# Layer 2's gates and branch products computed with tokens on the partitions, and turned back on the way into the output projection

## The reference

```python
def hybrid_layer(x, layer, norm_w, w_in, ..., w_branch, w_out, rel_bias):
    h = rms_norm(x, norm_w)
    p = h @ w_in                     # z, gate (4 x 2048 columns), the branches' inputs
    ...                              # four attentions of 4 heads: dsa, fox, diff, dilated
    for b in range(N_BRANCHES):      # 4
        y = branches[b].reshape(...) * jax.nn.silu(z_parts[b])          # 256 x 512
        term = jax.nn.sigmoid(g_parts[b]) * (y @ w_branch[b])           # 256 x 2048
        merged = term if merged is None else merged + term
    return x + merged @ w_out
```

## Time and profile before

| | |
|---|---|
| median of 3 runs | 2753.43 us (2752.55 to 2753.89) |
| span of the profiled execution | 2751.3 us, first to last instruction; what lies around it in a run is, by the median, 2.1 us; no other time is given for the profiled execution itself |
| PE busy | 2732.2 us, 99% of the span |
| PEld, DVE, ACT, POOL busy | 87%, 69%, 46%, 2% |
| TensorE's granted clock | 0.999 of full speed over the span |
| gates and what runs beside them | 2173.0 to 2557.3 us |
| 16 branch blocks | 2557.3 to 2649.4 us |
| 16 blocks of the projection | 2649.4 to 2738.8 us |

### The profile page before, as it was taken

The page is one execution under the profiler, slowest core; times in us unless marked ns, Lnnn a source line. Parts: engine busy times, 40 slices in busy tenths (PEclk is TensorE's granted clock), DMA queues, the critical chain, the costliest instruction groups (busy, mean ns, idle before and its releaser), DMA issues.

```text
span 2751.3 us, 40122 instructions
## 1 busy us (share of the span) xinstructions
PE 2732.2 (99%) x15856; PEld 2406.5 (87%) x15856; DVE 1898.5 (69%) x2111; ACT 1268.7 (46%) x1210; POOL 63.6 (2%) x113
## 2 busy tenths in 40 slices
PE   9999999999999999999999999999999999999998
PEld 8888888888888888888888888888888888888997
DVE  8685666777667879877777455765555766776686
ACT  6455457634645545544444333433333344443442
POOL 0000000000000000000000000000000000000100
PEclk9999999999999999999999999999999999999999
DMA  7764444565466555555555655555554566557853
GB/s 272 229 228 165 159 159 162 183 206 191 167 216 233 216 202 194 191 189 184 194 187 193 220 199 185 202 185 197 184 195 175 179 202 203 197 191 242 285 214 137
DMA packets 109476, 544.20 MB, mean 198 GB/s; under 512 B 11405, under 2 KB 25742, under 8 KB 54064
## 3 DMA queue, kind: packets, MB, share of 16 engines
q1 hardware_dynamic: 100128, 510.95, 53.0%
q0 software_dynamic: 9232, 31.57, 3.2%
HBM read 523.50 MB, written 23.04 MB: 199 GB/s over the span
## 4 chain that ended last, share of the span: by engine, by line
PE 91%; DVE 4%; ACT 2%; DMA 2%; issue 0%; SPq 0%; DVEq 0%; ACTq 0%
PE gemm L679 40%; PE gemm L682 21%; PE mix L679 6%; PE mix L1050 4%; PE mix L682 3%; PE gemm L733 2%; PE mix L1048 2%; PE gemm L735 2%; PE gemm L734 2%; DMA raw<-wstream 2%; DVE wlo L1726 2%; PE gemm L1050 1%; PE mix L657 1%; PE mix L656 1%; PE mix L655 1%; ACT whi L1228 1%
## 5 line engine op out<-in xcount | busy, mean ns | idle before, releaser
L1228 ACT ACTIVATE whi<-raw 128x2048 fp32r<-128x2048 f32 x466 | 891.2, 1913 | 1177.0 <-DMA raw<-wstream 1173.9
L1726 DVE TENSOR_TENSOR wlo<-raw,whi 128x2048 fp32r<-128x2048 f32 x465 | 1064.6, 2290 | 385.3 <-ACT whi L1228 384.2
L679 PE MATMUL gemm<-HX,whi 128*128 128x512 f32 x4864 | 1185.1, 393 | 2.0 <-DVE scratch L1751 0.7
L679 PEld LDWEIGHTS gemm<-HX,whi 128*128 128x128 f32 x4864 | 894.0, 188 | 174.4 <-issue 3.0
L682 PEld LDWEIGHTS gemm<-HX,wlo 128*128 128x128 f32 x4864 | 624.7, 191 | 21.5
L682 PE MATMUL gemm<-HX,wlo 128*128 128x256 f32 x4864 | 631.9, 283 | 0.0
L1751 DVE TENSOR_REDUCE arena<-gemm 128x256 f32<-128x512 f32 (+1 forms) x129 | 88.9, 689 | 177.6 <-PE gemm L679 177.4
L1050 PE MATMUL mix<-ACTX,whi 128*128 (+1 forms) x528 | 138.6, 392 | 0.3
L1050 PEld LDWEIGHTS mix<-ACTX,whi 128*128 128x128 f32 x528 | 97.0, 188 | 22.0 <-DVE XR L2312 2.9
L733 PE MATMUL gemm<-whi,HX 128*128 128x512 f32 x256 | 101.6, 397 | 1.6 <-DVE arena L1886 1.6
L679 PE MATMUL mix<-UX,whi 128*128 128x512 f32 x416 | 101.6, 392 | 0.0
(11 more groups left out here) (423 smaller groups left out, 2530.7 us busy)
## 6 DMA issues: line engine op xcount, KB each, us to landing
raw<-wstream SPq DMA_DIRECT2D x462, 1024.0 KB, 4.8
scratch<-gate_scratch POOLq DMA_DIRECT2D x12, 512.0 KB, 5.3
raw<-wstream SPq DMA_DIRECT2D x10, 512.0 KB, 6.2
gate_scratch<-scratch SPq DMA_DIRECT2D x32, 128.0 KB, 4.6
GL<-gate_scratch POOLq DMA_DIRECT2D x8, 512.0 KB, 5.3
gate_scratch<-arena SPq DMA_DIRECT2D x32, 128.0 KB, 4.7
bias_scratch<-row_scratch POOLq DMA_DIRECT2D x21, 192.0 KB, 5.2
raw<-wstream SPq DMA_DIRECT2D x12, 256.0 KB, 8.0
```

What stands on the lines that cost most here:

```text
L679: return pe.matmul(bank.rearrange("p (c t) -> p c t", c=2), whi[slot][:, w(k)], mx(k), start=k == 0, stop=k == total - 1)
L1228: f(whi[slot][:, :], raw[slot][:, :], ACT.Copy).then_inc(s["hi_ready"], 1)
L1726: tt(wlo[slot][:, :], raw[slot][:, :], whi[slot][:, :].bitcast(F32), ALU.subtract).then_inc(s["lo_ready"], 1)
```

## The change

The 64 gate blocks become 16 value groups: group k gives 512 features with tokens on the partitions, in banks `gate_bank`, which are the two gemm banks for even k and banks 4 and 5 of `M` for odd k. DVE copies a group's two banks out after its fourth block, and SP stores them in `gate2_d` as two transfers of 256 KB.

The 16 branch blocks also have tokens on the partitions (`YH` and `YL` stationary, 24 matmuls of 512 columns), and go by column quarters: quarter q is the four branches' blocks 4q to 4q + 3. So the gates come back in that order too (`gate2_back`), and a quarter of `merged` is complete after each fourth block. It then has tokens on the partitions, and the projection wants features there. DVE transposes its 32 x 32 blocks (two `transpose` instructions into `turned`), SP writes the four strips of 32 partitions to the scratch tensor `turn_d` in four transfers of 128 KB, waits until they have landed, and reads them back rearranged into `laid` (512 KB). ACT makes the high part of it (`turned_high`) and DVE the low part (`turned_low`), both beside the second block of the next quarter. Tokens then lie in the order strip, half, place; the moving operands of the projection are read in runs of 64, and DVE puts the tokens right as it adds the projection to the residual. The projection starts with three blocks taken together, chunks 0 to 11 first, then 12 to 15.

Cut to its core:

```diff
@@ V_GROUPS, stream_index
+V_GROUPS += tuple(range(B_G2, B_Y2, 4))
...
+    if isinstance(n, int) and B_Y2 <= n < B_O2:
+        return B_Y2 + N_Y2 * ((n - B_Y2) % 4) + (n - B_Y2) // 4
@@ sync
+            def strips(q):
+
+                sp.wait_ge(s["mg_t"], q + 1)
+                if q:
+                    sp.wait_ge(s["mg_l"], N_Y + q)
+                for a in range(4):
+                    sp.dma_start(turn_d[q, a].rearrange("b j x -> j b x"),
+                                 turned[32 * a:32 * a + 32, :].rearrange("j (b x) -> j b x", b=4)).then_inc(s["mg_out"], 16)
+                sp.wait_ge(s["mg_out"], 64 * (q + 1))
+                sp.dma_start(laid.rearrange("p (a x) -> p a x", a=4), turn_d[q].rearrange("a b j x -> (b j) a x")).then_inc(s["mg_in"], 16)
...
-            blocks(sp, B_G2, 4 * N_G, spill(1, 2 * N_G, use(B_G2)))
-            blocks(sp, B_Y2, N_BLOCKS - RING - B_Y2, reload)
+            for n in range(B_G2, B_Y2 + 1):
+                reload(n, n % RING, n // RING, 0, 0)
+                if n > B_G2 and (n - B_G2) % 4 == 0:
+                    spill2((n - B_G2) // 4 - 1)
+            for n in range(B_Y2 + 1, B_O2):
+                reload(n, n % RING, n // RING, 0, 0)
+                if (n - B_Y2) % 4 == 3:
+                    strips((n - B_Y2) // 4)
+            blocks(sp, B_O2, N_BLOCKS - RING - B_O2, reload)
@@ gpsimd
+            for i in range(4, 4 * N_Y2):
+                pool.wait_ge(s["y2_out"], i - 3)
+                gate2_back(i)
+                if i >= 12:
+                    pool.dma_start(XT2[:, quarter(i - 12), :], x2_d[:, quarter(i - 12), :]).then_inc(s["x2_back"], 16)
@@ tensor, values
-                    if b == 0:
-                        pe.wait_ge(s["evac_done"], u + t - 1)
-                    bank = gps[(u + t) % 2][:, :].rearrange("p (c f) -> p c f", c=4)
+                    if b == 0 and gate != 1:
+                        pe.wait_ge(s["evac_done"], u + t - (1 if gate < 1 else 3))
+                    if b == 0 and g == B_SUMS2:
+                        pe.wait_ge(s["head_rstd"], 4)
+                    bank = (gps[(u + t) % 2][:, :] if gate < 0 else gate_bank(g, t)).rearrange("p (c f) -> p c f", c=4)
@@ tensor, branch blocks
-                for c in range(4):
+                wh = whi[n % RING][:, :].rearrange("p (c k f) -> p k c f", c=4, k=4)
+                wl = wlo[n % RING][:, :].rearrange("p (c k f) -> p k c f", c=4, k=4)
+                for t in range(2):
+                    bank = M[:, 2 * (i % 2) + t, :].rearrange("p (c f) -> p c f", c=4)
                     for k in range(4):
-                        kk = 4 * (i // N_Y2) + k
-                        ins = mm3(M[:, 2 * (i % 2) + c // 2, (c % 2) * T:(c % 2 + 1) * T], cols(c * 4 + k),
-                                  YH[:, kk, :], YL[:, kk, :], n % RING, k == 0, k == 3)
+                        kk = 4 * (i % 4) + k
+                        yh, yl = YH[:, kk, cols(t)], YL[:, kk, cols(t)]
+                        pe.matmul(bank, yh, wh[:, k], start=k == 0, stop=False)
+                        pe.matmul(bank, yl, wh[:, k], start=False, stop=False)
+                        ins = pe.matmul(bank, yh, wl[:, k], start=False, stop=k == 3)
...
-            pair(B_O2, s["mg_l"], [(N_Y + i + 1, 4 * i + 4) for i in range(N_Y2)], hk, xk)
-            project(B_O2 + 2, N_O - 3, hk, xk)
+            for sem, k0, k1 in ((N_Y + 3, 0, 12), (N_Y + 4, 12, KT)):
+                pe.wait_ge(s["mg_l"], sem)
+                for b in range(3):
+                    ...
+                    ins = group(out_bank(b), range(k0, k1), KT, cols, hq, xq, n % RING, strips=True)
+            project(B_O2 + 3, N_O - 4, hq, xq, strips=True)
@@ scalar
+            for i in range(4 * N_Y2):
+                plain(B_Y2 + i, 1)
+                if 2 <= i < 4 * N_Y2 - 2:
+                    gate2(i + 2)
+                if i % 4 == 1 and i > 4:
+                    turned_high(i // 4 - 1)
+            plain(B_O2, 1)
+            turned_high(3)
@@ vector
+                if n == 3:
+                    if q:
+                        dve.wait_ge(s["mg_out"], 64 * q)
+                    ...
+                    for t in range(2):
+                        ins = dve.transpose(dst[:, t], src[:, t])
+                    ins.then_inc(s["mg_t"], 1)
...
+            for i in range(4 * N_Y2):
                 gated(i)
+                if i % 4 == 1 and i > 4:
+                    turned_low(i // 4 - 1)
                 plain(B_Y2 + i, 1)
-            for i in range(3 * N_Y2, 4 * N_Y2):
-                gated(i)
-                if i > 3 * N_Y2:
-                    merged_low(N_Y + i - 3 * N_Y2, 16, i - 3 * N_Y2 - 1, 4)
-                if i == 4 * N_Y2 - 1:
-                    merged_low(N_Y + N_Y2, 16, N_Y2 - 1, 4)
-                plain(B_Y2 + i, 1)
+            turned_low(3)
```

More of the change, by code:

```diff
@@ L693, in group, with project @@
                 return ins
-            def project(n0, count, mh, ml, fresh=None):
+            def project(n0, count, mh, ml, fresh=None, strips=False):
                 u0 = use(n0)
@@ L708, in body @@
                             pe.wait_ge(fresh[0], fresh[1] + q + 1)
-                        ins = group(gps[bank][:, :], ks, KT, cols, mh, ml, slot)
+                        ins = group(gps[bank][:, :], ks, KT, cols, mh, ml, slot, strips)
                     ins.then_inc(s["gemm_done"], 1)
@@ L735, in values @@
                         ins = pe.matmul(bank, xh, wl[:, k], start=False, stop=kk == KT - 1)
-                    if b == 3 and t == 0:
+                    if b == 3 and t == 0 and gate < 0:
                         ins.then_inc(s["v_half"], 1)
@@ L1786, in to_gates, with gate_values, take, to_ring @@
                 join(gates[0:56, :], gps[(u0 + j) % 2][0:56, :]).then_inc(s["evac_done"], 1)
-            def to_ring(layer, began):
+            def gate_values(k):
+                def take(n, u0, i, j):
+                    if n % 4 != (B_G2 + 3) % 4:
+                        return
+                    dve.wait_ge(s["gemm_done"], n + 1)
+                    for t in range(2):
+                        if k:
+                            dve.wait_ge(gate2_out[t], 16 * k)
+                        dve.tensor_copy(gring2[t], gate_bank(B_G2 + 4 * k, t)).then_inc(s["evac_done"], 1)
+                return take
+            def to_ring(began):
                 def take(n, u0, i, j):
@@ L2523, in _ @@
             dve.wait_ge(s["x2_back"], 64)
-            plain(B_O2, N_O, use(B_O2), residual(3, XT2), 3)
+            no_squares()
+            plain(B_O2, 3, use(B_O2), residual(3, XT2), 3)
+            plain(B_O2 + 3, N_O - 3, use(B_O2 + 3), residual(3, XT2, 3), 3)
             d = XT2[:, KT - 1, :]
```

176 lines of the change are left out of this document (112 added, 64 removed).

## The result

The median after the change is 2766.66 us (5 runs, 2765.01 to 2768.54), beside it before the change 2753.89 us: the ratio is 1.0047, 95% interval 1.0035 to 1.0060. The change makes the kernel 0.47% slower. The forecast was 2756 us, with a range that ended at 2766. The profiled execution took 2766.08 us, its span 2764.3 us.

A forecast was written before the change was run, and what follows sets the result against it. PE, busy 99% of the span, was taken as the bound. A gain of 13.4 us and waits of 16.1 us summed to +2.7: span 2754.0 us, median 2756.1, range 2746 to 2766.

The forecast's parts named there:

- the four places named: Where PE was to wait: branch blocks 8 and 12, the projection's start and its second pass.
- The gain: PE's gate blocks 8.3 us and branch blocks 5.1 us shorter, 13.4 us in sum.
- The transposes: DVE's two transposes per quarter, taken as 1.4 us, done 4.2 us after the quarter's fourth block.
- SP's stand: SP's four writes after the transposes, 0.35 us apart until 5.3, landed at 7.2 us after block 3.
- The load behind it: Weight load for block 8 goes out at 7.6 us, not 5.7, takes 7, not 5.0, landed at 14.7.
- PE's waits: PE waits 1.8 us before branch block 8, 4.9 before block 12, 2.4 before the projection.
- the 20.1 + 5 us of DVE a quarter: Branch blocks: DVE's work plus its standstill before the low part, 25 us per 21.8 us of PE.
- The clock: After long PE waits matmuls run at half speed, 0.45 us each, 4 to 5 us in all.
- rival 3: Slower by PE's half clock after waits, 4 to 5 us, 2760 to 2761; chance 0.12.
- After it: Projection: waits of 0.5 and 1.9 us at second and third block, 2.7 second pass, 1.9 fourth block.
- Rival 2: Slower by DMA crowding in the branch blocks: loads take 9 us, not 7, landing beyond 17; 2763; chance 0.25.
- Rival 1: The gain stays: DVE fits in the branch blocks, only a last chain of 3 to 5 us; 2744; chance 0.20.

The follow-up runs named there:

- e17: The changed kernel with four useless 512-column matmuls behind each of branch blocks 4 to 14, 10.0 us of PE work; 2766.7 us, ratio 1.0051.
- e4: The changed kernel with 12, 12, 8 and 8 useless matmuls ahead of PE's waits at branch blocks 8 and 12, projection start and second pass; 2766.4 us.
- e9: e8 with the last trip by SP, the third quarter's low part behind the last transposes, and the projection's first blocks in three passes; 2747.7 us, ratio 0.9982.
- e8: The changed kernel with the whole trip in POOL's queue and the high and low part one block later; 2755.6 us, ratio 1.0009.
- e7: The changed kernel with SP's next load ahead of its wait and read, and the high and low part one block later; 2760.1 us, ratio 1.0027.
- e16: The changed kernel with POOL's four residual pieces moved from the third quarter to the last one and after; 2766.3 us, ratio 1.0051.
- e14: The changed kernel with write wait and read by POOL (three quarters), later high/low parts, three projection passes, fourth projection block's split earlier; 2751.9 us, ratio 0.9997.
- e3: The changed kernel without transposes and trip through DRAM, high and low parts made from the merged quarter as it lies; 2745.5 us, ratio 0.9972.
- e5: The changed kernel with the whole trip (writes, wait, read) in POOL's queue, SP keeping the weight loads alone; 2762.2 us, ratio 1.0039.

## Why the prediction was wrong

The mechanism was right: the trip delays the load, ACT's high part and DVE's low part in this order, and PE waits at the four places named. Its sizes were not, and the one that failed is the time of the writes, 3.0 us a quarter. Each step against what was measured:

- **The gain.** Value matmuls stood 0.227 us apart, and the branch stage began at 2549.4 us, 7.9 earlier (forecast 8.3). Of the 5.1 us of the branch blocks only the first four's 1.3 shows: from block 4 on PE isn't on the chain, and in e17 10 us of extra work there cost nothing.
- **The transposes.** 1.30 us for two, taken as 1.4. They ended 3.9 us after block 3 (forecast 4.2).
- **SP's stand: the term that failed.** I took 3.0 us from the transposes' end to the landed writes. SP's timeline:

```profile
2571.38 0.33 SPq L512 DMA_DIRECT2D raw<-wstream  x1
2575.30 1.83 SPq L546 DMA_DIRECT2D turn_scratch<-arena  x4
2581.28 0.38 SPq L549 DMA_DIRECT2D arena<-turn_scratch  x1
2581.71 11.76 SPq L512 DMA_DIRECT2D raw<-wstream  x4
```

It was 6.0 us here, and 3.6, 5.5 and 3.6 in the other quarters: 6.7 more than four times 3.0. The fourth write, 0.44 to issue and not 0.35, landed 4.6, 2.2, 4.2 and 2.2 us after its issue began. I had reasoned that the weight load ahead of the writes would have landed by then. In the first quarter it had been issued 3.9 us before them and landed 7.0 us after its issue, between the last write's issue and its landing; a gates' piece, issued 2.3 us before the writes, was under way too. In the third quarter it was a gates' piece and one of the residual; in the second, with 2.2 us for the last write, one gates' piece alone.

By the Trainium skill ("DMA: Bandwidth & Descriptors", "Anatomy of one DMA") a write of 128 KB takes 2.3 us. That is an estimate from a fit that the page made on transfers issued by GpSimd, and these are SP's. The last write of the second and fourth quarters agrees, with 2.2 us; those of the other two, beside more transfers, took 4.6 and 4.2.

- **The load behind it.** Taken 7.1 us from issue to use; measured 7.1, 8.7 and 6.1. The high part was done 21.3 us after block 3's end, not 18.7, and DVE stood 7.7, 8.4, 7.8 and 6.7 us, not 5.
- **PE's waits.** Forecast 1.8, 4.9 and 2.4, measured 4.5, 5.0 and 3.2, start to start. The second pass began 99.7 us after block 3's end and not 92.0 (12 x 5.44 for the branch blocks, 12.5 for the first pass, 14.2 of waits). The loop shows what made up the 7.7 us. The writes are 6.7; the loads add 0.5 and the last read 0.2. About 1 us is a slip in my sum: by its own list the second quarter's transposes end 30.7 us after block 3, so 8.9 after their block and not 7.3. The list has DVE stand 1.4 us for block 5, which the 20.1 + 5 us of DVE a quarter leave out. Added round the loop, 26.5 us a turn, the list gives 93.0. That is 8.4 in all, less 0.7 in steps that were a little shorter. The measured turns are 29.3, 28.5 and 27.8.
- **The clock.** It was a rival with 4 to 5 us; the half clock took 7.8. But most of that ran inside the loop of DVE and SP, where PE had time to spare: without the slow matmuls behind block 8 (e4) the time stayed. It counts behind the last low part, where PE is on the path again: 8.1 us from there to the fourth block, and 6.8 in e9 and e4, which have no slow matmul there: 1.3 us, a difference between profiled executions that the medians are too coarse to confirm. So rival 3's mechanism was there, and its price was not 4 to 5 us. The Trainium skill's rule on the idle array ("TensorE: Matmul & The Clock Gate", part 1) is what the rows show around blocks 8 and 12: after idle times of 4.3 and 4.8 us the granted clock was 0.5, and it was 1.0 again after a few matmuls without a pause. What it costs depends on who is on the path.
- **After it.** From the second pass to the fourth block it took 8.1 us, forecast 6.1, and block 3's end was 0.5 later. 7.7 + 2.0 + 0.5 = 10.2; span measured less forecast is 2764.3 - 2754.0 = 10.3.
- **Rival 2, crowding.** Its sign came true: the load landed 17.4 us after block 3's end, beyond the 17 I had given. But it was late because it went out at 10.4 and not at 7.6, and took 7.1 as forecast. Transfers in flight beside them are what goes with the long writes (above; no run changed that alone), so crowding probably has a part in the time through them. By itself it isn't enough: e8 and e9 move 341 and 340 GB/s over 2571.1 to 2638 us with PE dense. e7 shows that a load pushed back into a full stretch stays late. Moving the residual away changed no time (e16).
- **Rival 1** can be had, by other queues and places for the same work: e9.

What stays open: why the writes took 6.0 and 5.5 us in two quarters and 3.6 in the others, of which only the company they had is shown; why e14 is slower than e9, and why the clock fell behind a wait of 2.3 us in e3 and not behind one as long in e9.

## What to carry to other kernels

When a wait is put into a queue that also feeds the path (here SP's weight loads), price the whole loop that it closes, from the wait round to the wait again, and compare that period with the bound engine's: the longer one is the time, and what is done to the other engine doesn't matter as long as it stays the shorter. Keep such a wait in a queue from which nothing urgent is issued, and ask for its result as late as the buffers allow; the two alone gave 11 of the 21 us back (e8), and with the last trip in SP's queue, which was idle by then, the third low part later still, and the projection in three passes it was 19 (e9). For transfers issued into a busy stretch take the time of a transfer behind others, not that of one alone.

## What the hardware showed unexpectedly

- Four 128 KB writes took 3.6 to 6.0 us to land from SP's queue, 7.0 to 8.8 from POOL's in the first three quarters of e5 and 4.8 in its last. In the third quarter of e9, behind POOL's own pieces of gates and residual, it was 12.7 us (POOL's timeline):

```profile
2623.75 2.20 POOL L704 DMA_DIRECT2D turn_scratch<-arena  x4 [1.34 <-DVE arena L2644]
2636.45 0.76 POOL L709 DMA_DIRECT2D arena<-turn_scratch  x1 [10.51 <-DMA turn_scratch<-arena]
```

- A 1 MB load behind another load and a read was usable after 13.4 us, where one takes 4.8 by the median.
- After a wait PE's clock fell to half and came back to full within the same block in the branch blocks. At block 8, after 4.3 us of idle time, it fell only behind the fifth matmul, and nine distances from start to start were longer (0.27 to 0.43 us). e4's fillers kept it up at block 8 and not at block 12, where the wait behind the fillers was still 4.7 us.
